# Three edits to a fused transformer kernel: start modulations as row products with queries first, branch products gated by banks, two softmaxes joined on TensorE

## What is computed

```python
# layer 0: modulations, from c and c_ctx
mod_l = split(silu(c) @ w_mod[0] + b_mod[0], 6)
mod_c = split(silu(c_ctx) @ w_mod[0] + b_mod[0], 6)
u_l = rms_norm(x, g) * (1 + mod_l[1]) + mod_l[0]
u_c = rms_norm(ctx, g) * (1 + mod_c[1]) + mod_c[0]
# differential attention: queries of x alone, keys and values of ctx and x
s = einsum("bqhpd,bkhpd->bhpqk", q, k) * 64 ** -0.5
p = softmax(s)
a = p[:, :, 0] - lam * p[:, :, 1]
o = einsum("bhqk,bkhe->bqhe", a, v)
# hybrid mixer: four branches
branch = einsum("nbsc,ncd->bsnd", ys, w_branch)
merged = sum(sigmoid(mg) * branch, axis=2)
```

## Time and profile before

| | |
|---|---|
| median of 3 runs | 1768.11 us (1767.32 to 1772.85) |
| the profiled execution | 1773.37 us |
| its span | 1771.6 us |
| mean granted TensorE clock | 0.959 |
| PE, PEld, DVE, ACT busy | 93%, 86%, 65%, 43% |
| read from HBM | 307.5 MB |

### The profile page before, as it was taken

The page is one execution under the profiler, slowest core; times in us unless marked ns, Lnnn a source line. Parts: engine busy times, 40 slices in busy tenths (PEclk is TensorE's granted clock), DMA queues, the critical chain, the costliest instruction groups (busy, mean ns, idle before and its releaser), DMA issues.

```text
span 1771.6 us, 29009 instructions
## 1 busy us (share of the span) xinstructions
PE 1645.2 (93%) x12050; PEld 1523.1 (86%) x12050; DVE 1155.8 (65%) x1566; ACT 761.9 (43%) x883; POOL 11.5 (1%) x25
## 2 busy tenths in 40 slices
PE   6899776999999889999999999999899999999997
PEld 6898644899999766899998999888889999999996
DVE  6668795567767866555557446665456665788876
ACT  2222244345434332356434235544333433667664
POOL 0000000000000000000001000000000000000000
PEclk8799878999999999999999889999999999999999
DMA  8246521237677422225567244323342444778783
GB/s 326 77 187 215 190 95 72 72 144 259 236 263 251 165 99 92 72 100 185 173 231 278 97 164 167 126 92 117 121 149 95 161 172 167 259 299 310 300 308 116
DMA packets 43511, 310.21 MB, mean 175 GB/s; under 512 B 5239, under 2 KB 5624, under 8 KB 6984
## 3 DMA queue, kind: packets, MB, share of 16 engines
q1 hardware_dynamic: 41760, 301.75, 46.3%
q0 software_dynamic: 1248, 5.72, 1.0%
q10 hardware_dynamic: 392, 1.12, 0.2%
HBM read 307.53 MB, written 1.05 MB: 174 GB/s over the span
## 4 chain that ended last, share of the span: by engine, by line
PE 76%; DVE 15%; ACT 4%; issue 3%; DMA 1%; ACTq 0%; SPq 0%; DVEq 0%
PE ps L627 16%; PE ps L629 15%; PE ps L628 15%; PE ps L633 4%; PE ps L635 4%; PE ps L634 4%; DVE macc L1871 4%; DVE wlo L1859 2%; ACT whi L1385 2%; PE ps L751 1%; PE ps L682 1%; PE ps L684 1%; PE ps L683 1%; PE ps L1250 1%; PE ps L700 1%
## 5 line engine op out<-in xcount | busy, mean ns | idle before, releaser
L1859 DVE TENSOR_TENSOR wlo<-raw,whi 128x2048 fp32r<-128x2048 f32 x218 | 497.9, 2288 | 292.3 <-ACT whi L1385 291.3
L627 PE MATMUL ps<-uhi,whi 128*128 128x256 f32 x1728 | 500.7, 290 | 16.1 <-DVE ulo L1901 4.2
L1385 ACT ACTIVATE whi<-raw 128x2048 fp32r<-128x2048 f32 x218 | 416.0, 1911 | 201.6 <-PE ps L629 157.2
L628 PE MATMUL ps<-uhi,wlo 128*128 128x256 f32 x1728 | 492.8, 285 | 0.0
L629 PE MATMUL ps<-ulo,whi 128*128 128x256 f32 x1728 | 492.6, 285 | 0.0
L627 PEld LDWEIGHTS ps<-uhi,whi 128*128 128x128 f32 x1728 | 335.7, 194 | 26.0 <-issue 18.0
L628 PEld LDWEIGHTS ps<-uhi,wlo 128*128 128x128 f32 x1728 | 336.0, 194 | 0.9 <-issue 0.7
L629 PEld LDWEIGHTS ps<-ulo,whi 128*128 128x128 f32 x1728 | 335.4, 194 | 0.0
L627 PE MATMUL ps<-hid_hi,whi 128*128 128x256 f32 x512 | 145.0, 283 | 2.1 <-ACTq L1558 1.6
L629 PE MATMUL ps<-hid_lo,whi 128*128 128x256 f32 x512 | 143.9, 281 | 0.0
L628 PE MATMUL ps<-hid_hi,wlo 128*128 128x256 f32 x512 | 143.8, 281 | 0.0
(11 more groups left out here) (462 smaller groups left out, 2845.2 us busy)
## 6 DMA issues: line engine op xcount, KB each, us to landing
raw<-weights_in SPq DMA_DIRECT2D x258, 1024.0 KB, 4.8
y<-weights_in SPq DMA_DIRECT2D x18, 1024.0 KB, 5.7
mstart<-mod_start_in SPq DMA_DIRECT2D x4, 2048.0 KB, 19.6
w1c<-cmp_w_in POOLq DMA_DIRECT2D x1, 2048.0 KB, 12.6
h<-x_in SPq DMA_DIRECT2D x1, 1024.0 KB, 8.0
ctx<-ctx_in SPq DMA_DIRECT2D x1, 1024.0 KB, 18.7
y<-decay_in ACTq DMA_DIRECT2D x1, 1024.0 KB, 4.8
out<-y SPq DMA_DIRECT2D x4, 256.0 KB, 2.6
```

The costliest lines, as they stand in the source:

```text
L627: mm(o, w0, x0, start=first, stop=False, **kw)
L628: mm(o, w1, x0, start=False, stop=False, **kw)
L1385: fn(whi[:, sl, :], raw_at(i) if n is None else raw[:, sl, :], ACT.Copy).then_inc(s("hi_ready"), 1)
L1859: tt(wlo[:, sl, :], raw_at(i) if n is None else raw[:, sl, :], f32(whi[:, sl, :]), ALU.subtract).then_inc(s("lo_ready"), 1)
```

## The change

**Start.** The even pairs are made the other way round: the two columns of `csil` are held and 256 columns of the weights are moved (`start_rows`, four pieces of 256 columns, the even pairs, and one of 128, the second tile of the last odd pair, so that VectorE's last weighing covers only the other 128 columns). The result is two rows; ScalarE copies them to `sq` (`copy_rows`), and TensorE turns each 128 of them into columns (`turn_rows`). The squares of x are summed behind the first piece, those of ctx behind the third. VectorE's reciprocal for x comes behind all four weighings. ScalarE takes the context's root right after its sum (into `hdn`), ahead of the first split, and splits chunks 1 and 2 ahead of the context's high half; VectorE likewise splits them ahead of the context's reciprocal, scaling and low half.

**Stream.** Query chunks come before key chunks, the context being needed from the fifth chunk. The modulations behind the first two chunks are gone; in the first MLP's output half there are ten instead of eight (behind chunks 1, 3, 5, 6, 7, 9, 10, 11, 13, 15).

**Branches.** The branch chunks signal their first half (`br_half`). VectorE gates each bank by itself as it comes, and each half of a product, and each gate chunk, waits only for its own bank.

**Softmaxes.** VectorE no longer touches `ebuf`. It scales two identity matrices by the reciprocals (`diag`), and TensorE multiplies both parts of `ebuf` by them, adding in PSUM: transposing, scaling and the sum in eight products of 128 columns.

```diff
+START_PIECES = ((0, 0, 256), (2, 0, 256), (4, 0, 256), (6, 0, 256), (7, 128, 128))
+START_BANKS = (0, 1, 2, 3, 6)
...
-    out = [mat("attn_w_qkv", (0,), c0 + 256 * j) for c0 in (D, 0, 2 * D) for j in range(4)]
+    out = [mat("attn_w_qkv", (0,), c0 + 256 * j) for c0 in (0, D, 2 * D) for j in range(4)]
...
-    after = {w: 1 for w in range(12)}
+    after = {w: 1 for w in range(2, 12)}
...
-    after.update({32 + w: 1 for w in range(1, 16, 2)})
+    after.update({32 + w: 1 for w in (1, 3, 5, 6, 7, 9, 10, 11, 13, 15)})
...
-            for j in range(0, START_TILES // 2, 2):
+            def start_rows(n):
+                j, c0, width = START_PIECES[n]
                 pe.wait_ge(s(f"start_loaded{j // 2}"), 16)
-                if j == 2:
-                    sum_squares("x", 4)
-                for m in range(2):
-                    for k in range(KT):
-                        w = k * 2 * P + m * P
-                        mm(ps[:, 7, 4 * j + 2 * m:4 * j + 2 * m + 2], mstart[:, j, w:w + P], csil[:, k, :], start=k == 0, stop=k == KT - 1)
...
+                for k in range(KT):
+                    w = k * 2 * P + c0
+                    ins = mm(ps[0:2, START_BANKS[n], 0:width], csil[:, k, :], mstart[:, j, w:w + width], start=k == 0, stop=k == KT - 1)
+                ins.then_inc(s("start_rows"), 1)
+
+            def turn_rows(n):
+                j, c0, width = START_PIECES[n]
+                pe.wait_ge(s("start_copied"), n + 1)
+                for m in range(width // P):
+                    tile = 2 * j + c0 // P + m
+                    ins = nc.tensor.transpose(ps[:, 7, 2 * tile:2 * tile + 2], start_row[0:2, 256 * n + m * P:256 * n + (m + 1) * P], ident[0:2, 0:2])
+                return ins
...
+            start_rows(0)
+            sum_squares("x", 4)
+            start_rows(1)
+            start_rows(2)
             sum_squares("ctx", 5, src=y)
+            turn_rows(0)
+            turn_rows(1)
+            start_rows(3)
+            start_rows(4)
+            for j in (1, 3, 5):
+                sum_weighted(j, range(2))
+            turn_rows(2)
+            turn_rows(3)
+            sum_weighted(7, range(1))
+            turn_rows(4).then_inc(s("mod_start"), 1)
             idle_work(6, 8)
...
                 for k in range(4):
-                    ins = nc.tensor.transpose(ps[:, 4 + u % 2, k * P:(k + 1) * P], ebuf[:, u % 2, 0, k * P:(k + 1) * P], ident)
+                    for p in range(2):
+                        ins = mm(ps[:, 4 + u % 2, k * P:(k + 1) * P], ebuf[:, u % 2, p, k * P:(k + 1) * P], diag[:, u % 2, p, :],
+                                 start=p == 0, stop=p == 1)
...
+            def branch_rows(t, mid):
+                n, g = divmod(t, 6)
+                def second_half():
+                    if mid:
+                        mid()
+                    pe.wait_ge(*((s("mg_free"), 4 * n + 4) if g == 4 else (s("br_free"), 4 * n + 2)))
+
+                pe.wait_ge(*((s("mg_free"), 4 * n + 3) if g == 4 else (s("br_free"), 4 * n + 1)))
...
                 if g < 2:
                     if n:
-                        pe.wait_ge(s("br_free"), 2 * n)
+                        pe.wait_ge(s("br_free"), 4 * n - 1 + g)
...
             squares("x", h)
             root("x", 4)
+            copy_rows(0)
             act.wait_ge(s("ctx_loaded"), 16)
             squares("ctx", ctx, y)
+            for n in range(1, 3):
+                copy_rows(n)
+            act.wait_ge(*nth("ctx", "sumsq", 1))
+            fn(hdn[:], ps[:, 5, 0:T], ACT.Sqrt, bias=eps, scale=1.0 / D).then_inc(s("std"), 1)
             split(0)
+            for n in range(3, 5):
+                copy_rows(n)
             high("x", y, uhi, mod_scale(0, 0, 0))
-            root("ctx", 5)
-            high("ctx", ctx, ctx_hi, mod_scale(0, 0, 1))
             for i in range(1, RING):
                 split(i)
+            high("ctx", ctx, ctx_hi, mod_scale(0, 0, 1))
...
             low("x", y, uhi, ulo, mod_scale(0, 0, 0))
+            for i in range(1, RING):
+                split(i)
+            dve.wait_ge(*nth("ctx", "std", 1))
+            chain(nc.vector.reciprocal(rstd[:], hdn[:]))
             prenorm("ctx", ctx, ctx, coef[:, 1])
             low("ctx", ctx, ctx_hi, ctx_lo, mod_scale(0, 0, 1))
-            for i in range(1, RING):
-                split(i)
...
-                a = chain.tick(ts(e0, e0, r[:, 0:1], None, ALU.mult))
-                b = chain.tick(ts(e1, e1, r[:, 1:2], small[:, 26:27], ALU.mult, ALU.mult))
-                dve.wait_ge(chain.sem, b)
-                tt(e0, e0, e1, ALU.add).then_inc(s("att_ready"), 1)
+                if u >= 2:
+                    dve.wait_ge(s("att_turned"), u - 1)
+                ts(diag[:, u % 2, 0, :], ident, r[:, 0:1], None, ALU.mult)
+                ts(diag[:, u % 2, 1, :], ident, r[:, 1:2], small[:, 26:27], ALU.mult, ALU.mult).then_inc(s("att_ready"), 1)
...
-                    dve.wait_ge(s("chunk_used"), i + 1)
-                    src = ps[:, 6:8, :].rearrange("p b (m t) -> p (b m) t", m=2)
-                    chain(stt(gated[:, a, :] if n else y[:, a, :], gated[:, a, :], 1.0, src, ALU.add, ALU.mult))
-                    dve.sem_inc(s("br_free"), 1)
+                    for half in range(2):
+                        dve.wait_ge(*((s("chunk_used"), i + 1) if half else (s("br_half"), 2 * n + g - 3)))
+                        b = slice(a.start + 2 * half, a.start + 2 * half + 2)
+                        stt(gated[:, b, :] if n else y[:, b, :], gated[:, b, :], 1.0, halves(ps[:, 6 + half, :]), ALU.add, ALU.mult)\
+                            .then_inc(s("br_free"), 1)
+                    dve.wait_ge(s("br_free"), 4 * n + 2 * (g - 4) + 2)
```

More of the change, by code:

```diff
@@ L394, in program @@
             atb = alloc(st, "atb", [2, 4, T])
+            diag = alloc(st, "diag", [2, 2, P])
         with ExitStack() as st:
@@ L646, in used, with tiles @@
                 ins.then_inc(s("chunk_used"), 1)
-            def tiles(i, bank_of, xs, kts=8, width=2, cols=T, k0=0, first=True, last=True, x_wait=None, between=None):
+            def tiles(i, bank_of, xs, kts=8, width=2, cols=T, k0=0, first=True, last=True, x_wait=None, between=None, half_done=None):
                 sl = i % RING
@@ L666, in tiles @@
                                         first and k == 0, last and k == kts - 1)
+                    if half_done and m == width // 2 - 1:
+                        ins.then_inc(s(half_done), 1)
                     if between and m == width // 2 - 1:
@@ L742, in _, with sum_weighted @@
             pe.wait_ge(s("c_silu"), 1)
-            for j in range(0, START_TILES // 2, 2):
+            def start_rows(n):
+                j, c0, width = START_PIECES[n]
                 pe.wait_ge(s(f"start_loaded{j // 2}"), 16)
-                if j == 2:
-                    sum_squares("x", 4)
-                for m in range(2):
-                    for k in range(KT):
-                        w = k * 2 * P + m * P
-                        mm(ps[:, 7, 4 * j + 2 * m:4 * j + 2 * m + 2], mstart[:, j, w:w + P], csil[:, k, :], start=k == 0, stop=k == KT - 1)
-            for j in range(1, START_TILES // 2, 2):
+                for k in range(KT):
[9 more added lines that the diff above has]
+                return ins
+            def sum_weighted(j, tiles_of):
                 pe.wait_ge(s("start_weighted"), (j + 1) // 2)
                 for w in range(2):
-                    for m in range(2):
+                    for m in tiles_of:
                         c = 4 * j + 2 * m + w
                         ins = mm(ps[:, 7, c:c + 1], start_acc[:, j // 2, w, m * P:(m + 1) * P], ones[:, 0:1], start=True, stop=True)
-            ins.then_inc(s("mod_start"), 1)
+            start_rows(0)
+            sum_squares("x", 4)
+            start_rows(1)
+            start_rows(2)
             sum_squares("ctx", 5, src=y)
+            turn_rows(0)
[8 more added lines that the diff above has]
+            turn_rows(4).then_inc(s("mod_start"), 1)
             idle_work(6, 8)
@@ L792, in _ @@
                 if g < 4:
+                    ins = tiles(i, lambda m, _: ps[:, b, m * T:(m + 1) * T], [lat], x_wait="x" if g == 0 else None)
+                elif g < 8:
                     ins = tiles(i, lambda m, x_i: ps[:, b + m, (1 - x_i) * T:(2 - x_i) * T], [lat, con_x],
[L795 to L797 removed]
+                                x_wait=("x", "ctx") if g == 4 else None)
                 else:
@@ L1108, in attend @@
                     nsa_values(u - 3)
+            def branch_rows(t, mid):
[5 more added lines that the diff above has]
+                pe.wait_ge(*((s("mg_free"), 4 * n + 3) if g == 4 else (s("br_free"), 4 * n + 1)))
+                used(tiles(I_BR + t, lambda m, _: ps[:, 6 + m // 2, (m % 2) * T:(m % 2 + 1) * T], [(yhi, ylo)], kts=MT, width=4, k0=MT * n,
+                           between=second_half, half_done="br_half"))
             for t in range(24):
@@ L1129, in _ @@
                 else:
```

(10 more changed lines are left out.)

20 lines of the change are left out of this document (11 added, 9 removed).

## The result

The changed kernel takes **1741.3 us** (median of four, 1741.2 to 1741.9) where the kernel before took 1769.4 beside it (four, 1767.3 to 1772.9): a ratio of 0.984 [0.983, 0.986]. The forecast was 1735, in a range of 1728 to 1751 and with 0.94 for faster. Sign and range held; the point was 6 us low. The profiled executions took 1773.4 and 1741.9, 31.5 us apart (spans 1771.6 and 1740.1), where the sum said 33.4.

The account below looks back on a forecast made before the run. TensorE, busy 93% of the span, was taken as the bound, with VectorE bounding query projections and attention. Terms 18.2 - 1.5 + 8.0 + 8.7 = 33.4 us took 1773.4 to 1740, and the median's 5.3 offset gave 1735; range 1728 to 1751.

Parts of the forecast that it names:

- Start: Kernel start: making the even pairs as rows lets normalization of x begin at about 47.2 us instead of 59.8, 12.6 saved.
- Rival (b): Start: the clock stays at 1.2 GHz, 64 us where the forecast has 46, 18 less gained, 1753 us; chance 0.06.
- Queries first: Query and key projections: query chunks first bring the first value chunk at 134.6 against 152.78, 18.2 us including the start's 12.6.
- Rival (e): One reordering does nothing, first products wait for something not moved; only 12.6 of 18.2 us gained, 1741; chance 0.02.
- Moved weighings: First MLP's output: two modulations added there cost 1.5 us, between 0.8 (only TensorE) and 4 (stalls at five chunks).
- Softmaxes: Attention: VectorE's passes shrink, TensorE becomes the bound, pairs with a weighing take 8.5 us; 8.0 us saved, between -8 and 12.
- Rival (a): Attention: diagonal products give back VectorE's saving, clock drops in two of eight pairs, 15.6 us each; 1749 us, chance 0.20.
- Rival (d): Attention wholly at 1.2 GHz: 43 us lost instead of 8 gained, 1786 us, slower; chance 0.03.
- Branches: Branch stage: gating bank by bank removes TensorE's five waits of 1.45 us and two of 0.73; 8.7 us saved.
- Rival (c): Branch stage: the halves come late in place of the gate, 3 of 8.7 us are left, 1741 us; chance 0.07.
- sum of 33.4: Whole kernel: 18.2 - 1.5 + 8.0 + 8.7 us saved, taking the profiled execution from 1773.4 to 1740.
- the 5.3 us: Last step of the forecast: the median of runs, 1768.1, lay 5.3 us below the profiled execution, so 1740 became 1735.

Follow-up runs that it names:

- experiment 3: Kernel before with only the new start's rows; keys still first, all weighings in old places, context's work in old order: 1757.7 us against 1772.0, ratio 0.9921.
- experiment 4: Changed kernel with the two moved modulations put back behind the first two query chunks, eight left in the first MLP's output: 1746.1 us, ratio to kernel before 0.9855.
- experiment 5: Changed kernel with the first MLP output's ten modulations placed otherwise, in two versions: one run of five, 1742.2 us; five pairs, 1740.2 us.
- experiment 1: Kernel before with only the softmax change (diagonal matrices multiplied by TensorE): 1762.4 us against 1772.0, ratio 0.9945.
- Experiment 6: Changed kernel with TensorE multiplying only the first softmax by its diagonal, the second's share left out, VectorE's work unchanged: 1731.9 us, ratio to kernel before 0.9777.
- Experiment 2: Kernel before with only the branch change (half signals, gating bank by bank): 1760.7 us, ratio 0.9941.
- experiment 8: Changed kernel with VectorE's late split one unit later and two more weighings moved to the first MLP's output: 1730.4 us; changed kernel beside it 1740.9.

## Why the prediction was right, and where 6 us went

**Start (12.6; 13.3).** Right, and by its own steps: the earlier trace rows's clock under 8 held columns carried over to 2 held columns, and the slow first piece was in the sum. The columns were ready at 45.9, where the sum has 46.0; the 0.7 more are the step from there to the normalization, 0.6 us where I had 1.2. Rival (b), the start at 1.2 GHz, did not come.

**Queries first (5.6 more; 4.2).** VectorE's periods and TensorE's key chunks came as worked out; the value products start at 135.24 for 134.6. From the normalization's start to them the forecast has 87.4 us. The table's profile has 88.7, with a granted clock of 0.94 from 70 to 84 us, and the changed kernel's second one 87.3, with 1.00: so 5.6 was the right size, and 4.2 is this execution's. Rival (e) is excluded. The forecast didn't part the order from the two moved weighings, and by the runs the order alone costs 3: experiment 3 has neither and is 13.7 early at unit 0; experiment 4 has the order without the moved weighings and is 10.6 early, with x normalized at the same time (46.28 and 46.26). At 3 us this is twice what the same code varies there. Keys first, TensorE waits 3.6 us for the context's low half; queries first with all weighings, it waits 5.8 in two for `modv`; with two of them gone, 1.7. Keys first with two weighings moved was not tried.

**Moved weighings (-1.5; -4.4).** This is the mis-sized term. I stood at 0.8 for TensorE alone and 4 with a stall of 0.6 at each of five chunks, and took the lower part of that range. What came is just past its end: TensorE's waits for `modv` of 2.5 us in four, its own records of some 0.8, and 0.6 in the MLP's first half, which I had not in the sum. I had VectorE's turn (6.2) against TensorE's (6.1) and the thin ring; of the stalls of 3 us at most that I drew from them I took 0.7, and 2.5 came. ScalarE's wait for raw weights rose from 9.7 to 26.9 us beside it, but experiment 5's pairs, with 12.3, lost more. Which part of the ring makes TensorE wait is not shown. A stage in which TensorE was full to the hundredth had no slack to be given.

**Softmaxes (8.0; 6.8).** The unit's products came as forecast (2.05 for 2.0), the pairs with a weighing too (8.6 for 8.5), and VectorE's two operations take 0.29 and 0.34 for my 0.25. Missing are the number of such pairs and the late ones: from unit 0 to unit 14 three pairs save 1.6, the one behind the slow start loses 0.4, and three late ones save 0.3 each for my 0.5. The stretch behind the attention gave 1.4 here and took 1.4 in the changed kernel's second profile; up to the norm before the MLP the two gain 6.8 and 6.4. With the same code there, experiment 1 gains 6.3, experiment 4 4.0 and the two of experiment 5 2.8 and 5.6. So 6.8 is the best of six profiles, and the term was sized too high by 1.2 to 5.2. Rival (a) came weakened: single pairs slowed by up to 2 us (10.64 in the changed kernel, 11.85 in experiment 4), not two of 15.6, with TensorE in a pair idle for 0.4 us only. Rival (d), the whole attention at 1.2 GHz, did not come. By the Trainium skill's rule on transposes (TensorE: Matmul & The Clock Gate, Part 4) the term was to be 10. The full clock did come: 1.00 in the windows with a weighing above, where the kernel before had 1.00 in one pair and 0.67 in the next, without a change in the pair's length:

```profile
246.70:256.90 10.20, 7.03 (x23) 5.02 (x24) 9.74 (x23) 4.41 (x12) 0.00 (x0) 0.67 0.32 104
```

But TensorE also became fuller. Experiment 6 parts the two to some degree: it has products in place of the transposes too, but half as many, and the granted clock fell to 0.79 and 0.67 in two of its pairs. So that no transposes were left is not enough here for the full clock. And the gain is capped by TensorE's own work, as experiment 6 shows, not by the clock.

**Branches (8.7; 9.8).** Every wait of the earlier trace rows is gone, 8.8 us, and one of 0.6 for the last bank is new: 8.2 net, as TensorE's idle time says. The other 1.5 is the same 1676 records in less time. Experiment 2 has it too (223.46 us busy), but so has experiment 1 (223.60) with the old gating; over the profiles of all kernels here the new gating is busy for 221.2 to 223.6 and the old for 223.6, 225.1 and 225.1. So it isn't shown to be this part's: what the gating gained for sure is 8.2, and the forecast was closer than the 9.8 says. Rival (c) is excluded.

**The point.** The sum of 33.4 was 1.9 too much: 2.9 from the weighings, 1.2 from the softmaxes and 0.7 from start and queries, less 1.1 from the branches and 1.8 in stages that the change doesn't touch. All of these are sizes in single profiles, and the 1.1 and the 1.8 may in part be luck of the execution. The greater part of the miss came from the last step: I carried over to the changed kernel the 5.3 us by which the profiled execution lay above the median. The changed kernel's profiled execution and its median are 0.5 apart. Had the sum been taken from the profiled execution alone, it would have said 1740. The 5.3 was a median of three: two of those runs belong to the five below 1768.2, and over all 24 runs of the kernel before the median is 1771.8, only 1.5 below the profiled execution. Beside experiment 8 the two kernels' medians are 31.2 us apart (1772.1 and 1740.9), close to the 31.5 of the profiled executions. What makes those five runs faster is open. Experiment 2 shows one candidate in the old start, 4.3 us of it, but none of the five has a profile.

## What to carry to other kernels

Before work is moved into a stage "with room", count the transfers that go along and look at whether the engine that sets the end is full there: here two weighings brought 7 to 9 us where VectorE was the bound and cost 4.4 where TensorE was. When work is taken off one of two engines that wait for each other in turn, look for the instruction that stands first in its queue without need: one split moved by a unit was worth 10.5 us, more than all the arithmetic saved. And when the profiled execution lies off a median of three runs, run more before the offset is carried over; a stage's length should be read from several profiles, of kernels that share its code, before a difference of 1 or 2 us is given to an edit.

## What was not expected of the hardware

- Products that hold two columns and move 256 bring the clock up and keep it: from 21.7 us on records of 256 columns take 0.23 us (3.72 for 16), and 64 of the 100 records up to 41.7 us hold two columns. In the changed kernel's second profile the first 16, which all do, already took 5.29 for 6.34. In the kernel before, two moved columns under 128 held ones let it fall to 0.50.
- The same start code differs by 4.3 us between two executions (experiment 2 and the kernel before): the squares of x take 5.35 for 6.42 us, the 96 narrow records behind them 15.93 for 18.02, the context's squares 5.10 for 6.30.
- Small products can lose it again: behind the one- and two-column records from 41.62 to 45.8 the sixteen records of the idle products took 6.63 us, and 5.4 to 6.6 in four other profiles with the same code. Once, with experiment 5's pairs, they took 3.72:

```profile
44.31 3.72 PE L645 MATMUL ps<-con 128*128 128x256 f32 x16
```

- In the attention of the kernel before, pairs of units granted 0.67 and 1.00 were equally long (10.2 us), for VectorE was the bound: the clock cost nothing there.
